# Final sums of a mixture-of-experts block: two expert rows of 64 tokens stacked on the 128 partitions

## The reference

```
ys = lax.map(expert_block, (xs, block_expert))        # each expert's output rows
ys = ys * slot_gate[:, None]                          # times the token's gate for it
moe = zeros.at[slot_tok].add(ys)                      # two rows for each token
x = x + gt2 * moe
return rmsnorm(x, g_final)                            # x * rsqrt(mean(x*x) + 1e-6) * g_final
```

## Time and profile before

| | |
|---|---|
| median of 3 runs | 1263.9 us (1263.22 to 1266.0) |
| the profiled execution, first to last instruction | 1263.3 us |
| TensorE busy (matmuls) | 1220.1 us, 97% |
| VectorE busy | 959.5 us, 76% |
| ScalarE busy | 681.5 us, 54% |
| GpSimd busy | 257.5 us, 20% |
| DMA, whole span | 344.36 MB, mean 273 GB/s |

### The profile page before, as it was taken

How to read it: one execution, slowest core, us unless ns; L and a number is a source line. 1 busy time by engine, 2 the same in 40 slices (tenths; PEclk the granted TensorE clock), 3 DMA queues, 4 the chain that set the end, 5 groups by cost and what they waited for, 6 DMA issues and landing times. The chain is left out here.

```text
span 1263.3 us, 18788 instructions
## 1 busy us (share of the span) xinstructions
PE 1220.1 (97%) x7332; PEld 1013.2 (80%) x7332; DVE 959.5 (76%) x1173; ACT 681.5 (54%) x819; POOL 257.5 (20%) x193
## 2 busy tenths in 40 slices
PE   4799999999999999999989999999999999999997
PEld 1799888888788887888778888888888888788883
DVE  1756554432578888666789999999999999999977
ACT  3932212111456666422256777777777777677734
POOL 0000000001100000100020634535355272622110
PEclk9899999999999999999989999999999999999999
DMA  9649844435566775431379999999999999999949
GB/s 380 252 178 311 286 138 142 170 121 169 185 221 185 156 189 133 151 110 51 137 264 358 379 386 392 375 389 380 382 385 377 385 375 395 382 363 378 384 150 359
DMA packets 96620, 344.36 MB, mean 273 GB/s; under 512 B 18522, under 2 KB 46866, under 8 KB 68883
## 3 DMA queue, kind: packets, MB, share of 16 engines
q1 hardware_dynamic: 75603, 311.91, 67.8%
q10 hardware_dynamic: 11696, 14.44, 3.9%
q0 software_dynamic: 9232, 16.80, 3.6%
HBM read 314.24 MB, written 39.34 MB: 280 GB/s over the span
## 5 line engine op out<-in xcount | busy, mean ns | idle before, releaser
L2262 DVE TENSOR_TENSOR w_low<-raw,w_high 128x2048 fp32r<-128x2048 f32 x128 | 291.7, 2299 | 6.0 <-ACT w_high L2194 5.1
L2194 ACT ACTIVATE w_high<-raw 128x2048 fp32r<-128x2048 f32 x128 | 240.8, 1908 | 4.9 <-PEq L1388 3.8
L2076 PE MATMUL p_gu<-w_high,x_high 128*128 128x512 f32 x504 | 202.5, 402 | 0.0
L2078 PE MATMUL p_gu<-w_high,x_low 128*128 128x512 f32 x504 | 197.2, 391 | 0.0
L2077 PE MATMUL p_gu<-w_low,x_high 128*128 128x512 f32 x504 | 196.3, 390 | 0.0
L2262 DVE TENSOR_TENSOR w_low<-arena,w_high 128x2048 fp32r<-128x2048 f32 x62 | 142.6, 2303 | 25.5 <-ACT w_high L2194 25.5
L2134 POOL DMA_INDIRECT y_rows<-arena,row x31 | 66.9, 2158 | 311.1 <-DVE arena L2293 309.6
L2194 ACT ACTIVATE w_high<-arena 128x2048 fp32r<-128x2048 f32 x62 | 118.2, 1906 | 0.0
L2078 PEld LDWEIGHTS p_gu<-w_high,x_low 128*128 128x128 f32 x504 | 94.6, 188 | 20.9
L2077 PEld LDWEIGHTS p_gu<-w_low,x_high 128*128 128x128 f32 x504 | 94.9, 188 | 18.0
L2076 PEld LDWEIGHTS p_gu<-w_high,x_high 128*128 128x128 f32 x504 | 95.2, 189 | 17.7
(11 more groups left out here) (426 smaller groups left out, 2532.1 us busy)
## 6 DMA issues: line engine op xcount, KB each, us to landing
raw<-in_w_gate SPq DMA_DIRECT2D x64, 1024.0 KB, 7.9
raw<-in_w_up SPq DMA_DIRECT2D x64, 1024.0 KB, 8.1
arena<-in_w_down SPq DMA_DIRECT2D x62, 1024.0 KB
raw<-in_w_ada SPq DMA_DIRECT2D x24, 1024.0 KB, 7.6
x<-qk_rows SPq DMA_DIRECT2D x6, 1664.0 KB, 8.3
raw<-in_w_chunks SPq DMA_DIRECT2D x9, 1024.0 KB, 5.7
qk_rows<-x SPq DMA_DIRECT2D x18, 512.0 KB, 2.6
mod<-x ACTq DMA_DIRECT2D x48, 128.0 KB, 3.2
```

What stands on the lines that cost most here:

```text
L2076: pe.matmul(dst, high, w_high, start=start, stop=False)
L2078: return pe.matmul(dst, low, w_high, start=False, stop=stop)
L2194: act.activation(x.high[i % SPLITS][:], x.raw[b][:, :], ACT.Copy).then_inc(high_ok, 1)
L2262: dve.tensor_tensor(x.low[i % SPLITS][:], x.raw[home(n, j)][:, :], x.high[i % SPLITS][:], ALU.subtract).then_inc(low_ok, 1)
```

## The change

`yy[i]` of tiles 1 to 7 is filled in another layout. The tile's 128 tokens are two groups j of 64; partitions 0-63 get the first expert's rows of the 64 tokens, partitions 64-127 the second's, and group j lies in column block j. Each is read with two DMAs, one for each half of the partitions (`stacked`), where one read both (`whole`, kept for tile 0). One matmul with 128x64 weights, two 64x64 diagonals above each other, multiplies both rows by their gates and adds them, and writes to PSUM partitions 64j to 64j+63. For that the gates are read once more in the stacked order: four DMAs of 64 partitions x 32 bytes into `half_gates`, on SP at the start of the expert stage, before its first weight load. GpSimd adds the two halves of the identity (`twice`), VectorE makes 14 weight matrices of 128x64.

`SUMMED` is tiles 1 to 7, `DIRECT` is tile 0 alone, the order is 0 to 7. The four PSUM homes take the streams of tiles 1 to 4 as soon as VectorE's first weight matrix is there, those of 5, 6, 7 after the rows of 3, 4, 5, when tile 1, 2, 3 is scaled. `AWAKE_END` is 12, `AWAKE_ROWS_IN` is gone. The core of the diff:

```diff
@@ main_experts, SP
             sp.dma_start(x.consts[:], a.route_c).then_inc(c_in, 16)
+            last.gates(sp)
             for n, j in order:
@@ finish
+    def gates(sp):
+        for c in range(2):
+            for j in range(2):
+                sp.dma_start(half_gates[c * HALF:(c + 1) * HALF, j, :], s.gates[j * HALF:(j + 1) * HALF, c, :]).then_inc(gates_in, 16)
     def sync(sp):
+        def whole(i, w, done):
+            rows = a.y_rows.rearrange("(c n) d -> n c d", c=2)
+            sp.dma_start(yy[i][:, :, w], rows[i * P:(i + 1) * P, :, w]).then_inc(done, 16)
+        def stacked(i, w, done):
+            for c in range(2):
+                rows = a.y_rows[c * N + i * P:c * N + (i + 1) * P, w].rearrange("(j n) d -> n j d", j=2)
+                sp.dma_start(yy[i][c * HALF:(c + 1) * HALF, :, w], rows).then_inc(done, 16)
         sp.wait_ge(q.all_rows, 1)
-        for i in split:
-            sp.dma_start(yy[i][:, :, left], rows[i * P:(i + 1) * P, :, left]).then_inc(...)
+        whole(0, left, y_columns[0])
+        stacked(1, left, y_columns[1])
+        stacked(2, left, y_in[2])
         sp.wait_ge(q.all_rows, 2)
-        for i in split:
-            sp.dma_start(yy[i][:, :, right], rows[i * P:(i + 1) * P, :, right]).then_inc(y_in[i], 16)
-        for i in SUM_ORDER[3:]:
-            sp.dma_start(yy[i], rows[i * P:(i + 1) * P]).then_inc(y_in[i], 16)
+        whole(0, right, y_in[0])
+        stacked(1, right, y_in[1])
+        stacked(2, right, y_in[2])
+        for i in range(3, NT):
+            stacked(i, slice(0, D), y_in[i])
@@ tensor
-        def rows(i):
+        def rows(i, h):
...
-                for k in range(2):
-                    total = pe.matmul(banks[i][:, h, :], diags[:, n, k, :], yy[i][:, k, h * 512:(h + 1) * 512], start=False, stop=(k == 1))
+            for j in range(2):
+                total = pe.matmul(banks[i][j * HALF:(j + 1) * HALF, h, :], diags[:, n, j, :], yy[i][:, j, h * 512:(h + 1) * 512], start=False, stop=True)
...
-        stream(SUMMED[0])
-        stream(SUMMED[1])
-        stay_awake(pe, x.p_gu[:, 0, :], s.ident[:], AWAKE_ROWS_IN)
-        pe.wait_ge(y_columns[0], 16)
-        stay_awake(pe, x.p_gu[:, 0, :], s.ident[:], AWAKE_ROWS_IN)
-        rows(SUMMED[0])
...
+        pe.wait_ge(diags_added, 1)
+        for i in SUMMED[:4]:
+            stream(i)
+        pe.wait_ge(diags_added, 2 * len(SUMMED))
+        for i in SUMMED:
+            if i in y_columns:
+                pe.wait_ge(y_columns[i], 32)
+                rows(i, 0)
+            pe.wait_ge(y_in[i], 64 if i == 2 else 32)
+            if i not in y_columns:
+                rows(i, 0)
+            rows(i, 1).then_inc(gathered, 1)
+            if i in (3, 4, 5):
+                stream(i + 2)
@@ vector
+        dve.wait_ge(gates_in, 16 * KD + 64)
+        dve.wait_ge(q.over_ready, OverTables.STEPS + 5)
         for n, i in enumerate(SUMMED):
-            for k in range(2):
-                dve.tensor_scalar(diags[:, n, k, :], s.ident[:], s.gates[:, k, i:i + 1], None, ALU.mult).then_inc(diags_added, 1)
+            for j in range(2):
+                dve.tensor_scalar(diags[:, n, j, :], twice[:], half_gates[:, j, i:i + 1], None, ALU.mult).then_inc(diags_added, 1)
```

More of the change, by code:

```diff
@@ L60 @@
 AWAKE_SUMS, AWAKE_MIX, AWAKE_CHOICE, AWAKE_RANK, AWAKE_LIST, AWAKE_ROWS = 4, 3, 14, 12, 24, 30
-DIRECT, SUMMED = (0, 2, 4, 7), (1, 3, 5, 6)
+DIRECT, SUMMED = (0,), (1, 2, 3, 4, 5, 6, 7)
 EARLY_CHOICE = 5
-AWAKE_END, AWAKE_ROWS_IN = 48, 22
-SUM_ORDER = (0, 2, 1, 4, 3, 5, 7, 6)
+AWAKE_END = 12
+SUM_ORDER = tuple(range(NT))
 class Counter:
@@ L2600, in finish @@
     last = Buffers()
+    HALF = P // 2
     yy = [y[:, :].rearrange("p (c n) -> p c n", c=2) for y in s.raw + s.late_raw + [s.xg_pair, s.y_pair]]
-    gains, diags = x.over_work, s.keep.rearrange("p (i k q) -> p i k q", k=2, q=P)
-    banks = {i: b for i, b in zip(SUMMED, (x.p_x[:].rearrange("p (c k) q -> p c (k q)", c=2), x.p_y[:], x.p_gu[:], x.p_hl[:]))}
+    gains, diags = x.over_work, s.keep.rearrange("p (i j q) -> p i j q", j=2, q=HALF)
+    homes = (x.p_y[:], x.p_gu[:], x.p_hl[:], x.p_x[:].rearrange("p (c k) q -> p c (k q)", c=2))
@@ L2604, in finish @@
+    banks = {i: homes[n % 4] for n, i in enumerate(SUMMED)}
+    half_gates, twice = t.sb("half_gates", [P, 2, NT]), t.sb("twice", [P, HALF])
     eps, half = t.sb("eps6", [P, 2]), t.sb("half6", [P, NT])
     ss, root, rstd, tmp = (t.sb(n, [P, NT]) for n in ("ss6", "root6", "rstd6", "tmp6"))
-    y_in, y_columns = [t.sem(f"y_in{b}") for b in range(NT)], {i: t.sem(f"y_columns{i}") for i in (0, 2)}
-    diags_added, gathered = t.sem("diags_added"), t.sem("gathered6")
+    y_in, y_columns = [t.sem(f"y_in{b}") for b in range(NT)], {i: t.sem(f"y_columns{i}") for i in (0, 1)}
@@ L2608, in finish @@
+    gates_in, diags_added, gathered = s.wo_in, t.sem("diags_added"), t.sem("gathered6")
     rooted, scaled, stored = t.sem("rooted6"), t.sem("scaled6"), t.sem("stored")
     halves = lambda x: x.rearrange("p (c n) -> p c n", c=2)
-    def sync(sp):
-        rows = a.y_rows.rearrange("(c n) d -> n c d", c=2)
-        left, right = slice(0, 512), slice(512, D)
+    left, right = slice(0, 512), slice(512, D)
+    def gates(sp):
+        for c in range(2):
+            for j in range(2):
+                sp.dma_start(half_gates[c * HALF:(c + 1) * HALF, j, :], s.gates[j * HALF:(j + 1) * HALF, c, :]).then_inc(gates_in, 16)
@@ L2624, in sync @@
-        for n, i in enumerate(SUM_ORDER[:NT - 1]):
-            sp.wait_ge(scaled, n + 1)
+        whole(0, right, y_in[0])
[3 more added lines that the diff above has]
+            stacked(i, slice(0, D), y_in[i])
+        for i in range(NT - 1):
+            sp.wait_ge(scaled, i + 1)
             sp.dma_start(a.out[i * P:(i + 1) * P, :], s.x1[:, i, :]).then_inc(stored, 16)
@@ L2628, in sync @@
             sp.wait_ge(scaled, NT + h)
-            sp.dma_start(a.out[last * P:(last + 1) * P, w], s.x1[:, last, w]).then_inc(stored, 16)
+            sp.dma_start(a.out[(NT - 1) * P:, w], s.x1[:, NT - 1, w]).then_inc(stored, 16)
         sp.wait_ge(stored, 16 * (NT + 1))
@@ L2634, in gpsimd @@
         steps.step(pool.memset(eps[:, 1:2], -0.5 * EPS))
+        steps.step(pool.tensor_tensor(twice[:], s.ident[:, 0:HALF], s.ident[:, HALF:P], ALU.add))
     def tensor(pe):
         def stream(i):
+            n = SUMMED.index(i)
+            if n >= len(homes):
+                pe.wait_ge(scaled, SUMMED[n - len(homes)] + 1)
             for h in range(2):
                 pe.matmul(banks[i][:, h, :], s.ident[:], s.x1[:, i, h * 512:(h + 1) * 512], start=True, stop=False)
-        def rows(i):
+        def rows(i, h):
             n = SUMMED.index(i)
-            pe.wait_ge(diags_added, 2 * (n + 1))
-            pe.wait_ge(y_in[i], 32 if i in SUM_ORDER[:3] else 16)
-            for h in range(2):
-                for k in range(2):
-                    total = pe.matmul(banks[i][:, h, :], diags[:, n, k, :], yy[i][:, k, h * 512:(h + 1) * 512], start=False, stop=(k == 1))
-            total.then_inc(gathered, 1)
-        pe.wait_ge(q.all_rows, 1)
-        pe.wait_ge(q.y_ok, NE)
-        stream(SUMMED[0])
-        stream(SUMMED[1])
-        stay_awake(pe, x.p_gu[:, 0, :], s.ident[:], AWAKE_ROWS_IN)
-        pe.wait_ge(y_columns[0], 16)
-        stay_awake(pe, x.p_gu[:, 0, :], s.ident[:], AWAKE_ROWS_IN)
-        rows(SUMMED[0])
[L2658 to L2662, removed]
+            for j in range(2):
+                total = pe.matmul(banks[i][j * HALF:(j + 1) * HALF, h, :], diags[:, n, j, :], yy[i][:, j, h * 512:(h + 1) * 512], start=False, stop=True)
+            return total
+        pe.wait_ge(diags_added, 1)
[12 more added lines that the diff above has]
+                stream(i + 2)
     def scalar(act):
@@ L2670, in scalar @@
             if i in DIRECT:
[L2671 removed]
+                act.wait_ge(diags_added, 2 * len(SUMMED) + 2)
                 src = halves(s.x1[:, i, :])
@@ L2683, in vector, with add @@
         stt = dve.scalar_tensor_tensor
-        def add(i, w=slice(0, D)):
+        def add(i, w):
             x1 = s.x1[:, i, w]
@@ L2700, in scale @@
             stt(x1, x1 if i in DIRECT else banks[i], rstd[:, i:i + 1], halves(gains[:]), ALU.mult, ALU.mult).then_inc(scaled, 1)
+        dve.wait_ge(gates_in, 16 * KD + 64)
+        dve.wait_ge(q.over_ready, OverTables.STEPS + 5)
         for n, i in enumerate(SUMMED):
-            for k in range(2):
-                dve.tensor_scalar(diags[:, n, k, :], s.ident[:], s.gates[:, k, i:i + 1], None, ALU.mult).then_inc(diags_added, 1)
+            for j in range(2):
+                dve.tensor_scalar(diags[:, n, j, :], twice[:], half_gates[:, j, i:i + 1], None, ALU.mult).then_inc(diags_added, 1)
         dve.wait_ge(s.const_in, 96)
-        left, right = slice(0, 512), slice(512, D)
         dve.wait_ge(y_columns[0], 16)
         add(0, left)
-        dve.wait_ge(y_columns[2], 16)
-        add(2, left)
         dve.wait_ge(y_in[0], 16)
         add(0, right)
```

(8 more changed lines are left out.)

2 lines of the change are left out of this document (removed).

## The result

Four runs of the changed kernel gave a median of 1277.2 us (1274.5 to 1283.5), beside 1263.95 for the kernel before on the same chip: ratio 1.0109, 95% interval 1.009 to 1.0127. **The change makes the kernel slower by about 1.1%, some 13 us.** The profiled execution spans 1277.1 us.

What follows compares the result with a forecast made beforehand. DMA was taken as the bound: from 1230.76, reads of 4.2 + 1.3 + 25.4 us end at 1261.6; stores of 10.15 and 0.33 give 1272.1, plus 0.6 to the median 1272.7 us. Range 1262.8 to 1278.3.

Steps and rivals of the forecast that it cites:

- A: Final reads: partial-partition transfers run at about 250 GB/s, giving 1272.7 us; chance 0.50.
- rival B: Final reads: pairs of engines share in lockstep throughout, 209 GB/s, giving 1278.2 us; chance 0.13.
- The rate of the reads: Final y_rows reads to 64 partitions: 248 GB/s, taken from line 585's swaps, between bounds of 209 and 411.
- Rival C: Final reads: engines drift apart onto different partition halves, the full 411 GB/s stay, giving 1263.1 us; chance 0.25.
- TensorE's rows: Final sums: column halves overlap, a tile's rows take 1.72 us; weight-width changes 0 to 1.3 us, taken as 0.
- D: TensorE's final row matmuls: column halves don't overlap, giving 1272.6 us; chance 0.04.
- The DMA is the floor: End of kernel before: last landing 1252.0, stores 10.15 us, some 0.3 more give 1262.5, so TensorE's queue can't be won.
- From the span to the median: Whole program: the median of the runs is 0.6 us above the profiled span.
- Issues: SP's queue at the end: 20 reads for 11 at 0.47 us each (0.97 at most); no bound.
- The expert stage: Its start: four gate DMAs delay the first weight load 1.3 to 1.9 us; cost taken 0, bounds 0 and 0.8.
- Clock and waits: Final sums: TensorE idles some 4 us, low clock costs 2, hidden by DMA; waiting for scaled tiles causes no stall.
- Tile 7's chain behind the last landing: Last tile: three engines need 5.5 us after reads end at 1261.6, until 1267.2; hidden by stores until 1270.5.

Runs made afterwards that it cites:

- x5: Changed kernel with the reads for partitions 64 to 127 sent over ScalarE's queue, the others left on SP's: 1271.0 us, ratio 1.0057.
- x7: Changed kernel with token and choice interleaved on all 128 partitions per read, plus extra matmuls filling TensorE's idle time: 1263.8 us, ratio 1.0002.
- x12: Kernel before with reads cut by expert row and left halves of five tiles instead of three read first: 1268.5 us, ratio 1.0036.
- x4: Changed kernel with token n's choice c on partition 2n + c, each group one read to all 128 partitions: 1264.1 us, ratio 0.9995.
- x9: Changed kernel with the same 64-partition reads, but each to every second partition: 1265.75 us, ratio 1.0007.
- x11: Kernel before plus only the four gate DMAs ahead of the expert stage's first weight load: 1265.7 us, ratio 1.0001.
- x6: Changed kernel with tiles 2, 4 and 6 each read whole by one 128-partition transfer: 1276.1 us, ratio 1.0101.

## Why the prediction was right, and where it was off

The forecast of 1272.7 us named the right cause (reads to part of the partitions, engines fully busy and delivering less) and the right side. The measured 1277.2 is at the upper end of the range: it lies outside A's own 1268.0 to 1275 and next to rival B (1278.2), which had a chance of 0.13.

- **The rate of the reads** is the term that was mis-sized. I took 248 GB/s from the swaps of line 585; it was 221 in the long stretch. With 221 the prediction's own sum gives 4.7 + 1.3 + 28.5 from 1230.76, reads in at 1265.3 (measured 1266.9), and an end at 1275.8 (measured 1277.1). The two windows didn't say which to take: in both, nearly all bytes were the swaps' (0.47 of 0.50 MB at 248 GB/s, 0.40 of 0.42 at 209). The measured rate lies between them, nearer to the lower. The step that failed is the choice of 248, and with it the low chance of B. The one sign that engines might drift out of each other's way was that the window with more swaps queued delivered more; in the profile after, the windows stay within 211 and 228 for 36 us. That is B's mechanism, at 221 instead of 209.
- **Rival C's condition** did not come about with the halves in one queue; with them in two (`x5`) half of it did.
- **TensorE's rows**: 1.72 us was the estimate. From start to start it was 1.77 when rows follow rows and 1.87 when a stream follows them, and a stream ahead of rows took 1.92 where I had 1.72 (`x7` above); two column halves do overlap, so D is out. For three, three and three such steps that is 1.2 us more than I had, near the upper bound I named (1.3).
- **"The DMA is the floor"** was wrong. I added 10.15 us of stores to the last landing and found 1262.5, near enough to 1263.3 to believe it. But from 1252.0 on the windows of the earlier trace rows and the row below hold only 3.7 of the 4.19 MB, so some 0.5 MB was stored ahead of the last landing, and the floor is about 1 us lower. And the floor isn't reached: the earlier trace rows has a share of 0.64 after 1256.5, and the last rows before start 1.2 us after the last read has landed because TensorE is still at the tile ahead. The constant tail and `x12` show it: at the full rate TensorE's work and its tail decide. The forecast hid the error, as for C I had 1261 by compute and 1262.5 by the floor, only 1.5 us apart; `x4` and `x9`, which meet C's condition, measured 1264.1 and 1265.75. With the reads at half the rate, as in the changed kernel, the DMA does decide.
- **From the span to the median**: the 0.6 us that I added is not a constant. Each run's time is some 1.8 us above its own span, and the profile is of one run; in the changed kernel the median is 0.1 above the profiled span.
- **VectorE**: 14 small weight matrices took 2.37 us (the row below), between 1.5 and 3.1, and were ready long before the first data. **Issues**: SP needs 0.61 us for a read to 64 partitions where I had 0.47; still no bound. **The expert stage**: four gate DMAs took 2.48 us for my 1.3 to 1.9; I took no cost, and none is shown (`x11`).
- **Clock and waits**: 0.50 from 1239 to 1244, tile 2's rows 3.68 us, as foreseen, and hidden behind the DMA. The wait for scaled tiles cost nothing here.
- Tile 7's chain behind the last landing was called hidden. It isn't quite: the last store goes out when VectorE is through at 1272.9, and the DMA share from 1272 to 1277 is 0.54.

The end of the kernel before, behind the windows of the earlier trace rows, and VectorE's weights in the changed kernel (their like before: the earlier trace rows):

```profile
1260.00:1263.30 3.30, 0.00 (x0) 0.00 (x0) 0.83 (x2) 0.00 (x0) 0.00 (x0) 0.77 0.72 281
```

```profile
1224.02 2.37 DVE L2728 TENSOR_SCALAR arena<-twice,half_gates 128x64 f32<-128x64 f32 x14 [0.76 <-issue]
```

## What to carry to other kernels

Bytes and number of the transfers did not tell the rate of these reads; which partitions they write did. Keep the partitions of one DMA spread over both halves of the 128: with two sources interleaved by a step of two instead of stacked, this layout cost nothing that could be measured (`x4`, `x9`). Before work is moved off an engine, count it again on the engine that ends last, in the time after its last input: here it was 17.4 us before and 18.1 after. And test a "floor" by its gaps (here a busy share of 0.64 near the end) and by what keeps its distance to the end when other things move.

## What was new about the hardware

- 32 neighbouring partitions are read as fast as 64, 223 and 221 GB/s (the former in one run); every second partition as fast as all 128, 414 and 411.
- Two queues, one for each half, reach 317 GB/s, and whole reads between half ones are slowed with them (`x6`, rows every 4.8 to 5.3 us).
- Changing between 128*128 and 128*64 matmuls costs 0.1 to 0.2 us each time: rows are followed after 1.77 us by rows and after 1.87 by a stream, a stream after 1.72 by rows of 128*128 and after 1.92 by rows of 128*64 (`x7`).
- The granted clock can fall to 0.50 in the first rows of the same final sums or stay at 1.00: they took 3.67 us in the profile of the kernel before, after 1.73 us of idle time, and 5.37 us in that of `x11`, after 1.88.
- Cutting the reads of the kernel before by expert row (`x3`) measured 0.17% faster, at the edge of what can be told; why is open, and no version beat the kernel before by more.
